# Two transformer blocks on one core: a first stage ordered by kinds of products, loads of x on two queues, and norm roots by GpSimd

## What is computed

```python
def rmsnorm(x, g):
    xf = x.astype(jnp.float32)
    y = xf * lax.rsqrt(jnp.mean(xf * xf, axis=-1, keepdims=True) + EPS)
    return (y * g.astype(jnp.float32)).astype(x.dtype)

n = rmsnorm(h, g_mix[l]);  proj = n @ w_in[l]               # start of block 1
n = rmsnorm(h, g_ffn[l]);  h = h + (silu(n @ w_gate) * (n @ w_up)) @ w_down
h = rmsnorm(h, g_final);   hn = rms_norm(h, attn_norm_g)    # start of block 2
hn = rms_norm(h, ffn_norm_g)                                # feed-forward of block 2
```

## Time and profile before

| | us |
|---|---|
| median of 3 runs (796.32 to 799.02) | 797.39 |
| the profiled execution: time / span of its instructions | 796.91 / 795.2 |
| PE busy | 757.7 (95%) |
| DVE / ACT / POOL busy | 530.1 / 421.0 / 73.9 |

### The profile page before, as it was taken

One profiled execution on the slowest core, in us unless ns is written; L12 is line 12 of the kernel. 1 busy time (PEld: TensorE's weight loads), 2 busy tenths in 40 slices (PEclk: granted clock), 3 DMA queues, 4 the chain that ended last, 5 costly groups with the idle time before them and its releaser, 6 DMA issues.

```text
span 795.2 us, 12591 instructions
## 1 busy us (share of the span) xinstructions
PE 757.7 (95%) x4989; PEld 680.0 (86%) x4989; DVE 530.1 (67%) x930; ACT 421.0 (53%) x799; POOL 73.9 (9%) x106
## 2 busy tenths in 40 slices
PE   2999999999999998999999998998989999999998
PEld 2999999989989987888888887997768888888886
DVE  5666465766555768777457757687877877547762
ACT  5356655455554446665345546468455555436551
POOL 8000000013022001000000003301500000000000
PEclk9999999999999999999999999999999999999999
DMA  9887636334433465564656563643234655665521
GB/s 289 237 262 236 164 68 185 107 107 116 150 107 134 159 212 164 181 206 167 211 179 192 187 202 98 214 146 114 102 119 145 212 185 186 212 196 175 168 97 54
DMA packets 108410, 132.04 MB, mean 166 GB/s; under 512 B 4267, under 2 KB 97513, under 8 KB 108352
## 3 DMA queue, kind: packets, MB, share of 16 engines
q1 hardware_dynamic: 106048, 126.56, 49.9%
q0 software_dynamic: 2304, 4.68, 2.6%
HBM read 129.39 MB, written 1.84 MB: 165 GB/s over the span
## 4 chain that ended last, share of the span: by engine, by line
PE 58%; DVE 8%; ACT 2%; issue 2%; POOL 1%; POOLq 0%; DVEq 0%
PE B L1480 23%; PE B L1457 19%; PE B L1462 10%; PE B L1441 5%; DVE LO L902 3%; ACT HI L510 1%; POOL SGC L465 1%; DVE AA L908 0%; PE B L1487 0%; PE B L1616 0%; DVE TMP L1358 0%; ACT SGC L830 0%; DVE NW L918 0%; ACT AA L514 0%; DVE ST L1177 0%
## 5 line engine op out<-in xcount | busy, mean ns | idle before, releaser
L902 DVE TENSOR_TENSOR LO<-RAW,HI 128x1024 fp32r<-128x1024 f32 x240 | 282.5, 1212 | 118.1 <-ACT HI L510 117.6
L510 ACT ACTIVATE HI<-RAW 128x1024 fp32r<-128x1024 f32 x240 | 237.8, 1040 | 60.1 <-PE B L1480 55.3
L1457 PE MATMUL B<-AA,HI 128*128 128x512 f32 x704 | 243.8, 399 | 2.6 <-DVE SGC L1191 2.1
L1480 PE MATMUL B<-HI,AA 128*128 128x512 f32 (+1 forms) x800 | 211.6, 350 | 6.4 <-DVE AA L1374 3.8
L1441 PE MATMUL B<-AA,HI 128*128 128x256 f32 (+1 forms) x992 | 186.0, 289 | 3.5 <-DVE LO L902 1.7
L1462 PE MATMUL B<-AA,LO 128*128 128x256 f32 x704 | 183.2, 281 | 0.0
L1480 PEld LDWEIGHTS B<-HI,AA 128*128 128x128 f32 x800 | 141.5, 190 | 26.3 <-DVE AA L1374 4.2
L1441 PEld LDWEIGHTS B<-AA,HI 128*128 128x128 f32 (+1 forms) x992 | 156.4, 193 | 5.7 <-DVE LO L902 2.1
L1457 PEld LDWEIGHTS B<-AA,HI 128*128 128x128 f32 x704 | 126.8, 188 | 27.9 <-DVE SGC L1191 2.7
L1441 PE MATMUL B<-AA,LO 128*128 128x256 f32 (+1 forms) x496 | 141.4, 285 | 0.0
L1462 PEld LDWEIGHTS B<-AA,LO 128*128 128x128 f32 x704 | 132.9, 189 | 8.1
(11 more groups left out here) (276 smaller groups left out, 639.0 us busy)
## 6 DMA issues: line engine op xcount, KB each, us to landing
RAW<-in_w_in SPq DMA_DIRECT2D x30, 1024.0 KB, 6.2
RAW<-in_w_gate SPq DMA_DIRECT2D x22, 1024.0 KB, 5.3
RAW<-in_w_up SPq DMA_DIRECT2D x22, 1024.0 KB, 5.3
RAW<-in_w_down SPq DMA_DIRECT2D x22, 1024.0 KB, 5.0
RAW<-in_w_in SPq DMA_DIRECT2D x9, 512.0 KB, 6.4
RAW<-in_w_attn_out SPq DMA_DIRECT2D x4, 1024.0 KB, 5.3
RAW<-in_w_o SPq DMA_DIRECT2D x4, 1024.0 KB, 5.0
RAW<-in_w_out SPq DMA_DIRECT2D x4, 1024.0 KB, 5.2
```

The lines of the kernel that those rows point to most:

```text
L510: e.activation(pieces(HI, NSPL, i, k), pieces(RAW, NRAW, i, k), ACT.Copy).then_inc(split_hi, 1)
L902: e.tensor_tensor(pieces(LO, NSPL, i, k), pieces(RAW, NRAW, i, k), pieces(HI, NSPL, i, k), ALU.subtract).then_inc(split_lo, 1)
L1457: return e.matmul(dst[:, :], hi[:, t, c0:c0 + 128], flatten(AA[:, ch + t, :, :]), start=(t == 0), stop=(t == nk - 1))
L1480: x = e.matmul(dst, a, w[:, t, c0:c0 + n], start=(first and t == 0 and k == 0), stop=(last and t == nk - 1 and k == 2))
```

## The change

- x's two pieces of token half 0 go over SP's queue with the gain g_mix as two rows of 512 between them; token half 1 goes over ACT's queue. SP issues weight unit 0 in two halves when the first piece has landed, and units 1 to 3 when all of x has.
- POOL first fills `ones`, then `ident`. PE multiplies ones by ones 8 times into an unused bank, spreads the gain over 128 partitions by two matmuls of one row (into banks 2 and 3), and multiplies ones 10 times more.
- DVE multiplies three of the four pieces of x by the gain before the root is there, and makes one mean for both token halves. The inverse root of all five row norms is one instruction of GpSimd, `tensor_tensor` with pow and exponent -0.5; the other norms stay with DVE's Newton steps. Scaling is shared: DVE does t = 0, ACT t = 1.
- The key product goes by kinds: for the first four chunks all high by high, then high by low, then low by high; then the other four chunks.
- In `last_pair` into block 2, `turned` of the second half now stands ahead of the HI and LO of unit 73. In `ffn`'s first step `hi(g + 3)` and `lo(g + 3)` stand where they do in the other ten. G2 waits for the third step of the first feed-forward. The scaling of X (L451) waits for the diagonals. `lo(U_TWO + 2)` is no longer in two parts between the steps of the roots.
- Semaphores of the gates are merged, which moves nothing.

```diff
+            for h in range(2):                                  # SP
+                e.dma_start(X[:, 0, halves(h)], A["x"][0, 0:128, halves(h)]).then_inc(x_in[h], 16)
+                if h == 0:
+                    e.dma_start(GAIN[0:128:64, :], A["g_mix"][0, :].rearrange("(a n) -> a n", a=2)).then_inc(row_in, 16)
+            e.wait_ge(x_in[0], 16)
...
+                if i == 0:
+                    e.dma_start(dst[:, 0:4, :], src[:, 0:4, :]).then_inc(unit0_in, 16)
+                    e.dma_start(dst[:, 4:8, :], src[:, 4:8, :]).then_inc(raw_in[0], 16)
+                    for h in range(2):
+                        e.wait_ge(x_in[2 + h], 16)
...
+            def root(n, dst, src):                              # POOL
+                e.wait_ge(mean_sb, n)
+                e.tensor_tensor(dst, src, ROOT[:, :], ALU.pow).then_inc(root_sb, 1)
...
             gain(1, A["attn_norm_g_2"][0, :])
+            root(2, ST[:, 6:8], ST[:, 4:6])
...
             e.wait_ge(mix_lo, 8)
+            e.wait_ge(fg_sb, 6)
             e.tensor_tensor(G2, GB[:, 0, :], GB[:, 1, :], ALU.mult).then_inc(gain2, 1)
...
+            root(3, ST[:, 6:8], ST[:, 4:6])
+            root(4, ST[:, 26:28], ST[:, 24:26])
+            e.wait_ge(root_sb, 3)
             e.wait_ge(squares_sb, 16)
             e.wait_ge(final_x, 4)
+            e.wait_ge(diag_sb, 4)
             for t in range(2):
                 e.tensor_scalar(X[:, t, :], TOK[:, t, :], ST[:, 6 + t:7 + t], None, ALU.mult).then_inc(normal_x, 1)
...
+            e.wait_ge(root_sb, 1)                               # ACT
+            for h in range(2):
+                e.wait_ge(gained_sb, 2 + h)
+                e.activation(TOK[:, 1, halves(h)], TOK[:, 1, halves(h)], ACT.Copy, scale=ST[:, 7:8]).then_inc(scaled_act, 1)
+                if h == 0:
+                    hi(0, 0)
+                    for t in range(2):
+                        turned(t, B[5 + t], 0, t)
             hi(0, 1)
+            for t in range(2):
+                turned(2 + t, B[5 + t], 4, t)
             hi(1)
...
+            e.wait_ge(gain_pe, 1)                               # DVE
+            for t, h in ((0, 0), (1, 0), (1, 1)):
+                e.wait_ge(x_in[2 * t + h], 16)
+                e.tensor_tensor(TOK[:, t, halves(h)], X[:, t, halves(h)], B[2 + h][:, :], ALU.mult).then_inc(gained_sb, 1)
+            e.wait_ge(squares_sb, 4)
+            e.scalar_tensor_tensor(ST[:, 4:6], ST[:, 0:4:2], EPS, ST[:, 1:4:2], ALU.add, ALU.add).then_inc(mean_sb, 1)
+            e.wait_ge(root_sb, 1)
...
-                    if h == 1 and split is not None:
-                        lo(split)
                     if targets:
                         for t in range(2):
                             turned(n + 2 * h + t, B[5 + t], 4 * h, t)
+                    if h == 1 and split is not None:
+                        lo(split)
...
-                own.step(rsqrt(ST[:, 6:8], ST[:, 4:6], 2))
-                own.wait()
+                e.wait_ge(root_sb, n)
                 diagonals(ST[:, 6:8])
...
+            def idle(n):                                        # PE
+                for _ in range(n):
+                    e.matmul(B[7][:, 0:128], ones[:, :], ones[:, :], start=True, stop=True)
...
+            for h in range(2):
+                if h == 0:
+                    turns(0)
+                for k, (w, a) in enumerate(((hi, AH), (hi, AL), (lo, AH))):
+                    if k == 0:
+                        e.wait_ge(split_hi, h + 1)
+                        e.wait_ge(turn_hi, 2 * h + 2)
+                    elif k == 1:
+                        e.wait_ge(turn_lo, 2 * h + 2)
+                    else:
+                        if h == 0:
+                            turns(1)
+                        unit_ready(U_KEYS, h)
+                    for c in range(2):
...
```

More of the change, by code:

```diff
@@ L497, in _ @@
             mean(1, bufs[1][:, 0:256], bufs[2], bufs[0])
+            root(5, ST[:, 6:8], ST[:, 4:6])
         @block.scalar
@@ L623, in turned_weights, with gates @@
                 e.activation(PT[:, s % 2, :], B[5 + s % 2][:, :], ACT.Copy).then_inc(pturn_sb, 1)
-            def gates(dst, u, pe, done):
+            def gates(dst, u, first):
                 for i in range(4):
@@ L629, in gates @@
                         ch = 2 * i + c
-                        e.wait_ge(pe, ch + 1)
-                        e.activation(dst[:, ch, :], B[c][:, 0:S], ACT.Tanh, scale=0.5).then_inc(done, 1)
+                        e.wait_ge(gate_pe, first + ch + 1)
+                        e.activation(dst[:, ch, :], B[c][:, 0:S], ACT.Tanh, scale=0.5).then_inc(gate_tanh, 1)
                         yield
@@ L759, in _ @@
                     squares(2 * t, X[:, t, :], scrap, h)
+                for t in range(2):
+                    turned(12 + 2 * h + t, B[5 + t], 4 * h, t)
                 if h == 1:
                     hi(U_TWO + 1)
-                for t in range(2):
-                    turned(12 + 2 * h + t, B[5 + t], 4 * h, t)
                 for t in range(2):
@@ L1225, in _ @@
             lo(U_FF1 + 1)
[L1226 removed]
+            factor(8, 2)
             ffn(U_FF1, 0, 1)
@@ L1488, in turn, with turns @@
                 x.then_inc(turn_pe, 1)
-            e.wait_ge(setup, IDENT)
-            for t in range(2):
-                for h in range(2):
-                    e.wait_ge(scaled_sb, 2 * t + h + 1)
-                    turn(2 * t + h, TOK[:, t, halves(h)], 5 + h)
+            def idle(n):
+                for _ in range(n):
+                    e.matmul(B[7][:, 0:128], ones[:, :], ones[:, :], start=True, stop=True)
+            e.wait_ge(setup, ONE)
+            idle(8)
+            e.wait_ge(row_in, 16)
+            for h in range(2):
+                take(2 + h, scaled_sb, 4)
+                x = e.matmul(B[2 + h][:, :], ones[64 * h:64 * h + 1, :], GAIN[64 * h:64 * h + 1, :], start=True, stop=True)
+            x.then_inc(gain_pe, 1)
+            idle(10)
+            e.wait_ge(setup, IDENT)
+            def turns(h):
+                e.wait_ge(scaled_sb, 2 * h + 2)
+                turn(2 * h, TOK[:, 0, halves(h)], 5)
+                e.wait_ge(scaled_act, h + 1)
+                turn(2 * h + 1, TOK[:, 1, halves(h)], 6)
             def keys(i, br, c):
                 take(c, keys_sb, 2 * br + c + 1)
-                stationary(i, 128 * c, B[c][:, 0:S], 0, c == 0, (turn_lo, 3, 4) if br == 0 and c == 0 else None).then_inc(keys_pe, 1)
+                stationary(i, 128 * c, B[c][:, 0:S], 0, c == 0).then_inc(keys_pe, 1)
             def values(i, br, t):
@@ L1502, in values @@
                 moving(i, 0, 256, B[t][:, 0:256], 0, t, t == 0).then_inc(vals_pe, 1)
-            for c in range(2):
-                keys(U_KEYS, 0, c)
+            hi, lo = view(HI, U_KEYS), view(LO, U_KEYS)
+            for h in range(2):
+                if h == 0:
[11 more added lines that the diff above has]
+                    for c in range(2):
+                        if h == 0 and k == 0:
+                            take(c, keys_sb, c + 1)
+                        for t in range(4 * h, 4 * h + 4):
+                            x = e.matmul(B[c][:, 0:S], w[:, t, 128 * c:128 * c + 128], a[:, t, :], start=(h == 0 and k == 0 and t == 0),
+                                         stop=(h == 1 and k == 2 and t == 7))
+                        if h == 1 and k == 2:
+                            x.then_inc(keys_pe, 1)
             e.wait_ge(rows_in, 192)
```

147 lines of the change are left out of this document (63 added, 84 removed).

## The result

| | before | changed |
|---|---|---|
| median of 4 runs, us | 796.99 (796.32 to 799.02) | 785.71 (784.86 to 786.61) |
| the profiled execution: time / span | 796.91 / 795.2 | 784.86 / 783.1 |
| PE busy | 757.7 (95%) | 763.5 (97%) |

PE has 40 instructions more, the ones products (36) and the gain's four passes, so its busy time grew while the time fell.

The account below looks back on a forecast made before the run. PE, busy 95% of the span, was taken as the bound, so only its idle times count. Terms −5.3 −3.0 −2.5 −0.9 +0.3 = −11.4 gave 785.5 for the profiled execution, 786.0 for the median, range 782 to 791.

Parts of the forecast that it names:

- First stage, −5.3: Start to unit 1's first matmul: earlier x, small gain and short root move it from 26.27 to 20.95.
- the rival that was kept apart: First stage: PE stays at half speed longer, costing +1.7 to +2.9; 788, chance 0.18.
- The sentence on x: First stage: all of x taken as landed by 6.2, called two thirds of the way from 9.29 to 3.92.
- the shift is kept: Behind the first stage PE is the bound for 100 us, so the 5.3 gained there stays.
- First feed-forward, −3.0: Start of the first feed-forward: −1.5 from earlier diagonals, −1.5 from gate adds ahead of two LO halves.
- Into block 2, −2.5: Passage into block 2: `turned` placed first removes PE's 2.56 wait behind its last transposes.
- Second feed-forward, −0.9: Second feed-forward: PE's wait for the gate's banks at 619.12, 0.73 plus 0.17, goes.
- Scaling of X, +0.3: POOL's scaling, now after the diagonals, stands beside more LO halves and may hold DVE; +0.3 taken.
- The rival of the port: Into block 2: POOL's scaling of X holds unit 74's LO up to 3.3, costing +2.4; 788.4, chance 0.07.
- The rival of a slow power: All roots: a power of 4.0 loses the whole gain, 799, chance 0.07; of 1.8 gives 789.3, chance 0.06.
- the formula as written: Loss for a power e above 0.4: first stage e, first feed-forward e−2, block 2 2e−0.9, second feed-forward e−2.1.
- First call: First stage: POOL's first root may load code, priced at 3.52 us; 789.5, chance 0.03.

Follow-up runs that it names:

- the second profile: The changed kernel itself, with no further edit, run and profiled once more beside later experiments; 783.87 us, ratio 0.9825.
- the late kind: Executions, not an edit: PE's clock rises only after the first eight ones products, gain ready at 6.9 to 7.4; the changed kernel's repeat, 783.87 us, was one.

## Why the prediction was right

The four places where the sum had its gain gave 11.65 of the 12.1 in the first profile, in place of 11.7. The terms inside them fared less well.

- **First stage, −5.3.** It measured 4.93 and 5.48 in the two profiles. The terms were off both ways. The mean came at 7.82 instead of 9.1, since POOL's ones were ready at 1.07 and not 1.6, the gain's passes ran in 1.19, and the three multiplications took 1.88. The power took 0.71 instead of 0.4. Then the rival that was kept apart came true in part: the first 16 passes at half speed, 3.65 where the second profile has 2.15. The end of the stage was seen rightly, PE's last group at 19.7 and unit 1 at 20.95 behind its LO; measured, 20.1 and 21.34. What I did not draw from it is that the order of the product is then hidden: DVE's last LO halves hang on the second turns, and these stand behind the first two groups. The sentence on x had a slip: two thirds of the way from 9.29 to 3.92 is 5.7 and not 6.2. It changed nothing, since the mean waited for the gain. The stage is the largest part of the gain and was not taken apart fully: of its 4.9 the root is some 1.2, the ones products 1.9 to 2.4 at unit 1's start, and holding the weights back and the order by kinds nothing; what x's two queues, the small gain, the early multiplications and ACT's share of the scaling are worth stays open.
- **0.7 more by 127.9.** PE waited 1.01 there before and 0.37 now. It is for a DVE instruction behind the HI and LO of a weight unit whose load ended a wait of 2.15 on ACT before, and 1.50 now. The sentence "the shift is kept" held, and 0.7 that no term had came on top. That it depends on where the loads land and not on the edit I didn't test: of the 13 profiles of the changed kernel and its variants, nine have 0.27 to 0.37 here and four 1.01 to 1.10, as before.
- **First feed-forward, −3.0.** 3.15 measured. The sum was right and its split was not: I gave 1.5 to the early diagonals and 1.5 to the order of the LO halves. The runs show the second as nothing, once the diagonals are early. And for the first, late G2 alone does it, and the short root alone all but 0.20.
- **Into block 2, −2.5.** 2.58, and 2.56 came back when the order was undone. The roots there are worth 1.8 (the wait for unit 74's LO with Newton steps). I had counted them only as slack; without them 1.8 of the −2.5 would go again, behind LO of unit 74.
- **Second feed-forward, −0.9.** 0.99; the short root alone gives it, and so does the order alone (184.93 each).
- **Scaling of X, +0.3.** Nothing on PE, and 0.2 on DVE: three LO halves in 3.79, where three in the first stage of the same profile take 3.57. The rival of the port is off: no LO was held by POOL's 4.70, which itself was the slower one, while the mean of two columns was held by G2 in each of the three profiles with G2 there (2.37, 2.38, 2.36). So of the rule of the Trainium skill that was cited ("SBUF — State Buffer", "SBUF: two separate sides"), that whoever starts first holds the other for its whole instruction, the row at 299.33 agrees and the row at 490.29 does not.
- **The other side.** The rival of a slow power had break-even at a root of about 3.6. With five powers a root takes 3.4, and the kernel stands at 0.9987 of the one before, which can't be told from no change. By the formula as written (e = 3.0) the loss is 10.0 of the 11.4, so 796.0; measured, 796.63. That it fits so well is in part luck, since the profiled execution lost 13.0 to the changed kernel's, with half-speed stretches that the formula doesn't have.
- **First call.** The first power took 0.71, as long as the second (0.72), and nothing stands idle ahead of it but the wait for the mean: nothing is seen to be loaded at the first. The Trainium skill's some 6 us for the first call of a freshly loaded kernel ("GPSIMD Engine Reference", 2.1 Instruction dispatch) does not show for this instruction.
- **The stretches in block 2 and at 229.** Price 1.3 to 1.5 each, given as 1.7; they came and went in both directions and nearly cancelled, which is luck: in the second profile neither moved, and the gain was 12.9.
- **The range.** The 784.3 at its foot is for the profiled execution; for the median the best first stage gives 784.8. No reading hangs on it.

## What to carry to other kernels

When two edits both shorten the way to the same wait, take each alone away before giving either its share: here late G2 or the short root was enough for the spread's wait, and the early diagonals or the order of the LO halves for the gate's. A large rewrite (the product by kinds) was worth nothing, because what PE won by starting early it lost waiting for DVE. When the last thing of a stage is on another engine, follow that engine's chain back before you give a price to an order on the busy one. A 0.7 us instruction on an idle engine in place of a 2 us chain on a busy one is a good trade as long as the price stays under the slack; measure that price by doing it several times. And read two profiles of a kernel before you explain a difference of 1.5 us in a stretch that no edit touches.

## What the runs showed of the hardware

- GpSimd's power on 128x2 takes 0.68 to 0.73, alone or in a row of five; from the end of the mean on DVE to the start of the next instruction 0.90 on ACT and 0.84 on DVE.
- The granted clock shows 1.00 in the windows from 4 to 8 in every run, though in those of the late kind PE's rows there are at half speed (four passes 2.08 instead of 1.19). At the start of a trace the rows' own durations tell the speed, the column does not.
- With the same eight ones products ahead, the clock rose before the gain's passes in seven profiles (1.13 to 1.39 for the four) and behind them in five (2.07 or 2.08).
- A wait of PE of 1.67 at 229 was followed by a stretch at half speed in 8 of 13 profiles, worth 1.5, and by none in 5; the wait of 2.56 into block 2 by none before and by some in the one run that brought it back.
- POOL and DVE beside each other: a 128x2 mean on DVE took 2.38 beside POOL's product of two operands, while LO halves beside POOL's scaling took 1.26 (1.19 in the first stage), and the scaling itself grew from 3.29 to 4.82 each.
